# Attention in two rounded halves: value products on split probabilities, and transposed probabilities evacuated piece by piece

## The reference, cut to what matters

```
logits = einsum(q, k_selected) / 8 + bias        # float32
p      = softmax(logits)                         # over the kept keys
out    = einsum(p, v_selected)                   # 64 values per head
```

## Time and profile before

| | us |
|---|---|
| runs (three) | 911.77, 914.68, 911.13; median 911.77 |
| profiled execution | 911.06 |
| its span | 909.2 |
| TensorE busy | 876.1 (96%) |
| VectorE busy | 562.5 (62%) |
| ScalarE busy | 412.4 (45%) |
| GpSimd busy | 362.5 (40%) |

### The profile page before, as it was taken

The page is one execution under the profiler, slowest core; times in us unless marked ns, Lnnn a source line. Parts: engine busy times, 40 slices in busy tenths (PEclk is TensorE's granted clock), DMA queues, the critical chain, the costliest instruction groups (busy, mean ns, idle before and its releaser), DMA issues.

```text
span 909.2 us, 18143 instructions
## 1 busy us (share of the span) xinstructions
PE 876.1 (96%) x6495; PEld 786.8 (87%) x6495; DVE 562.5 (62%) x1119; ACT 412.4 (45%) x1204; POOL 362.5 (40%) x537
## 2 busy tenths in 40 slices
PE   4999999999999999999998999999999999998998
PEld 4989887899999899999997997676797668998998
DVE  4537777899989988899740377756553137534111
ACT  6546671335556765675445455433342225421200
POOL 1544534249542954594669241630010105401310
PEclk9999999999999999999999999999999999999999
DMA  8220212100103020312050446653135434241422
GB/s 262 68 71 20 62 36 90 47 25 24 48 24 122 31 82 25 122 42 71 24 163 13 141 123 191 155 132 105 36 93 163 122 124 152 94 126 59 134 82 71
DMA packets 79422, 81.33 MB, mean 89 GB/s; under 512 B 20234, under 2 KB 68026, under 8 KB 79082
## 3 DMA queue, kind: packets, MB, share of 16 engines
q1 hardware_dynamic: 77722, 74.97, 27.3%
q0 software_dynamic: 1616, 5.25, 2.3%
HBM read 62.85 MB, written 17.34 MB: 88 GB/s over the span
## 4 chain that ended last, share of the span: by engine, by line
PE 62%; issue 13%; DVE 8%; DMA 7%; POOL 7%; ACT 2%; SPq 1%; DVEq 0%; POOLq 0%; ACTq 0%
PE psum L1999 12%; PE psum L1132 11%; PE psum L1996 7%; PE psum L1102 7%; DMA index_keys_T<-in_cache_ikt,index_page_rows 6%; PE psum L1088 4%; PE psum L1156 3%; PE psum L1198 3%; DVE flag L1788 3%; POOL w_low L461 3%; PE psum L1895 3%; PE psum L1067 2%; PE psum L1073 2%; PE psum L1071 2%; PE psum L1879 1%
## 5 line engine op out<-in xcount | busy, mean ns | idle before, releaser
L1999 PE MATMUL psum<-w_high,xT_high 128*128 128x256 f32 x720 | 205.1, 285 | 5.4 <-ACT stage L1582 2.3
L1999 PE MATMUL psum<-w_low,xT_high 128*128 128x256 f32 x720 | 202.6, 281 | 0.0
L1999 PE MATMUL psum<-w_high,xT_low 128*128 128x256 f32 x720 | 202.3, 281 | 0.0
L1788 DVE TENSOR_SCALAR_CACHE_REDUCE flag<-scores,candidate 128x384 f16<-128x384 f32 (+2 forms) x192 | 181.7, 946 | 6.9
L461 POOL TENSOR_TENSOR w_low<-w_raw,w_high 128x256 fp32r<-128x256 f32 (+1 forms) x168 | 122.7, 766 | 72.3 <-ACT w_high L1475 63.1
L1999 PEld LDWEIGHTS psum<-w_high,xT_high 128*128 128x128 f32 x720 | 128.2, 178 | 8.3 <-ACT stage L1582 2.5
L1999 PEld LDWEIGHTS psum<-w_low,xT_high 128*128 128x128 f32 x720 | 128.4, 178 | 2.3
L1999 PEld LDWEIGHTS psum<-w_high,xT_low 128*128 128x128 f32 x720 | 128.1, 178 | 2.4
L785 ACT ACTIVATE prob<-psum,neg_max 128x1024 f32<-128x1024 f32 (+7 forms) x64 | 47.5, 742 | 131.8 <-DVE neg_max L1005 131.8
L1996 PE MATMUL psum<-xT_high,w_high 128*128 128x384 f32 (+3 forms) x312 | 102.1, 327 | 1.6 <-DVE xT_low L1715 1.2
L1996 PE MATMUL psum<-xT_high,w_low 128*128 128x384 f32 (+3 forms) x312 | 99.7, 320 | 0.0
(11 more groups left out here) (299 smaller groups left out, 1847.1 us busy)
## 6 DMA issues: line engine op xcount, KB each, us to landing
w_raw<-in_w_main SPq DMA_DIRECT2D x40, 512.0 KB, 3.8
page_keys<-in_cache_kt SPq DMA_DIRECT2D x64, 128.0 KB, 2.6
page_values<-in_cache_v SPq DMA_DIRECT2D x64, 128.0 KB, 2.2
x_rows<-in_x_prompt SPq DMA_DIRECT2D x8, 512.0 KB, 5.8
x_res<-in_x_prompt SPq DMA_DIRECT2D x32, 128.0 KB
out<-y_rows SPq DMA_DIRECT2D x32, 128.0 KB
hgate_spill<-stage SPq DMA_DIRECT2D x16, 128.0 KB
ho_spill<-ho_rows SPq DMA_DIRECT2D x4, 512.0 KB, 3.9
```

The costliest lines, as they stand in the source:

```text
L1788: dve.tensor_scalar(JK[:, 0:w], sc, threshold(k), None, op, ALU.add, accum_out=CNT[:, k:k + 1]).then_inc(s["dve_chain"], 1)
L1999: last = pe.matmul(ps(BANK[n], w, rows(i)), x[:, k, row0(i):row0(i) + rows(i)], ww[:, sl, k, 0:w], start=first, stop=final)
```

## The change

The values are loaded per 128 rows in two halves of four blocks and split into a high part (rounded to fp32r by ScalarE) and a low part (the rest, by VectorE), which lie side by side, low then high, 128 columns for a key head. The transposed probabilities are evacuated in pieces, one for each PSUM bank: for tiles 7 to 4 blocks 0 to 3 from bank 4 and the others from bank 5; for the tiles below one piece, from bank 4 or 3 by turns. For each piece ScalarE writes the high part and VectorE the low part, PSUM minus the high part. No head is shared out by parity any more. For each block TensorE multiplies the high probabilities with low and high values (128 columns) and the low probabilities with the high values (64 columns), in fp32r. Bank 7 now holds four heads, so half a tile is put out at a time: VectorE adds the two parts (a reduction) and multiplies by the inverse row sums.

For room: two probability buffers in place of three, outputs in the loop in bank 1 alone in place of 1 and 3, other addresses, the mix blocks 0 to 4 one to three heads later, and the first two mix loads wait for the value products of the upper four tiles, because the second half of the values lies where they go.

The diff, cut to its core:

```diff
@@ -70,11 +70,17 @@
 SOFT_AT = MASK_AT[-1]
 VALUES_AT = [SOFT_AT + x for x in (6, 7, 8, 9, 11, 12, 14, 15)]
 
-SHARED_FROM = SOFT_AT
+PIECES = []
+for _m in range(NT * AH):
+    _t = NT - 1 - _m // AH
+    PIECES += [(_m, 4, 0, 4), (_m, 5, 4, _t + 1)] if _t >= 4 else [(_m, (4, 3)[_m % 2], 0, _t + 1)]
...
 
 ORDER = [7, 6, 5, 4, 3, NT, 2, 1, 0]
-MIX_AT = [34, 36, 39, 42, 45, 48, 53, 60]
+MIX_AT = [37, 39, 41, 43, 46, 48, 53, 60]
 OUT_AT = [41, 43, 45, 47, 49, 51, 52, 54, 55, 58, 63]
 HIGH_AT = {35: 0, 45: 1}
 
@@ -139,7 +145,7 @@
 OUTS += [(1, 3), (1, 4), (1, 5), (0, 8), (1, 6), (1, 7), (1, 8)]
 OUTS += [(v, x) for v in (2, 3) for x in range(NT + 1)]
 IN_LOOP = len(OUT_AT)
-OBANK = [(1, 3)[y % 2] if y < IN_LOOP else (0, 2, 1, 3)[(y - IN_LOOP) % 4] for y in range(len(OUTS))]
+OBANK = [1 if y < IN_LOOP else (0, 2, 1, 3)[(y - IN_LOOP) % 4] for y in range(len(OUTS))]
 OPREV = [max([m for m in range(y) if OBANK[m] == OBANK[y]], default=-1) for y in range(len(OUTS))]
 OEND = [max(y for y, o in enumerate(OUTS) if o[0] == v) + 1 for v in range(NUO)]
...
@@ -308,7 +314,8 @@
                                ("intra", [2, 2, P], F32), ("ho_rows", [NT, P], F32))
         QD, _ = over(_e - NT * P * 4, ("q_decayed_ref", [T], F32))
         assert _e <= cur[0], (_e, cur[0])
-        AO, PB, _e = over(I0, ("attn_out", [NT + 1, 512], F32), ("prob", [3, T], F32))
+        AO, PB, PTL, _e = over(I0, ("attn_out", [NT, 512], F32), ("prob", [2, T], F32), ("pT_low", [2, NT, P], F32R))
+        assert _e <= cur[0]
...
+
+
+        VA, BH, PTH, _e = over(H0, ("values_low_high", [4, KVH, 2, HD], F32R), ("bias_high", [AH, NEAR], F32R),
+                               ("pT_high", [2, NT, P], F32R))
         assert _e <= cur[0], (_e, cur[0])
+        VB, _ = over(S0 + SCW * 2, ("values_low_high_2", [4, KVH, 2, HD], F32R))
+        VHL = (VA, VB)
+        RA, _ = over(H0, ("values_raw", [4, KVH, 2, HD], F32))
+        RB2, _ = over(S0 + SCW * 2, ("values_raw_2", [4, KVH, 2, HD], F32))
+        VRAW = (RA, RB2)
 
         PSA = ctx.enter_context(nc.psum_tensor("psum", [P, 8 * 512], F32))
...
@@ -508,6 +521,12 @@
             for g, page in enumerate(pages_):
                 sp.dma_start(KP[x][:, :, g * P:(g + 1) * P], cache_kt[bass.ds(page, 1)].rearrange("a d j k -> (a d) j k"))\
                     .then_inc(s[f"key_pages_in{x}"], 16)
+
+        def load_values(sp, half):
+
+            for b in range(4):
+                t = 4 * half + b
+                sp.dma_start(VRAW[half][:, b, :, 0, :], v_prompt[0, 0, t * P:(t + 1) * P]).then_inc(s["values_in"], 16)
 
         def sp_last_unit(sp, q):
...
@@ -559,6 +578,8 @@
 
             def load_mix(x):
                 i = ORDER[x]
+                if x == 0:
+                    sp.wait_ge(s["attn_values_done"], NA // 2)
                 ge(sp, s["mix_transposed"], 2 * (x - 1))
                 ge(sp, s["mix_attn_ready"], x - 1)
                 for dst, src in ((HOR, d_ho), (HGR, d_gh), (AGR, d_ga)):
...
@@ -584,13 +605,16 @@
                     load_res(y + 2)
 
             store_keys(sp, NT - 1)
+            sp.wait_ge(s["q_rows_transposed"], NT)
+            sp.wait_ge(s["k_rows_transposed"], NT)
+            sp.wait_ge(s["k_out0"], 16 * 4)
+            sp.wait_ge(s["k_out1"], 16 * 4)
+            load_values(sp, 1)
             for n in range(2, 2 * SB):
                 load_key_pages(sp, n)
             for x in range(4):
                 sp.wait_ge(s[f"rows_out{x}"], ALLS[x])
             sp.wait_ge(s["ho_out"], 16 * NG)
-            sp.wait_ge(s["k_out0"], 16 * 4)
-            sp.wait_ge(s["k_out1"], 16 * 4)
             for b in range(4):
                 load_value_pages(b)
             sp.wait_ge(s["sample_hgrn_normed"], 1)
...
             sp.wait_ge(s["early_outputs_stored"], 48)
+            for b in range(4, SB):
+                load_value_pages(b)
             load_mix(0)
             load_mix(1)
-            for b in range(4, SB):
-                load_value_pages(b)
             sp.wait_ge(s["sample_values_done"], SB - 1)
             load_weights(sp, NU)
...
@@ -773,26 +798,33 @@
                 elif kind == "mix":
                     mix_high(act, b)
 
+            def values_high(half):
+                act.wait_ge(s["values_in"], 64 * (half + 1))
+                act.activation(VHL[half][:, :, :, 1, :], VRAW[half][:, :, :, 0, :], ACT.Copy).then_inc(s["values_high_ready"], 1)
+
             for side in SIDE[-1]:
                 sample(*side)
+            values_high(0)
             act.wait_ge(s["ho_out"], 16 * NG)
             for m in range(NA + 1):
                 if m < NA:
                     t, h = tile(m), m % AH
                     w = P * (t + 1)
                     act.wait_ge(s["max_ready"], m + 1)
-                    ge(act, s["probs_transposed"], m - 2)
-                    act.activation(PB[:, m % 3, 0:w], ps(2 * (m % 2), w), ACT.Exp, scale=-1.0, bias=NB[:, h:h + 1],
+                    ge(act, s["probs_transposed"], sum(len(PIECES_OF[x]) for x in range(m - 1)))
+                    act.activation(PB[:, m % 2, 0:w], ps(2 * (m % 2), w), ACT.Exp, scale=-1.0, bias=NB[:, h:h + 1],
                                    accum_out=RS[:, t % 2, h:h + 1]).then_inc(s["probs_ready"], 1)
                 m1 = m - 1
-                if m1 >= 0 and not by_dve(m1):
-                    w = P * (tile(m1) + 1)
-                    act.wait_ge(s["probs_transposed"], m1 + 1)
+                for x in PIECES_OF[m1] if m1 >= 0 else ():
+                    _, bank, b0, b1 = PIECES[x]
+                    act.wait_ge(s["probs_transposed"], x + 1)
                     ge(act, s["attn_values_done"], m1 - 1)
-                    if m1 == 0:
+                    if x == 0:
                         act.wait_ge(s["final_state_out"], 32)
-                    act.activation(PTS[:, m1 % 2, :, :].rearrange("p b t -> p (b t)")[:, 0:w], ps(4, w), ACT.Copy)\
-                        .then_inc(s["probs_T_act_ready"], 1)
+                    act.activation(PTH[:, m1 % 2, b0:b1, :].rearrange("p b t -> p (b t)"), ps(bank, (b1 - b0) * P), ACT.Copy)\
+                        .then_inc(s["probs_T_high_ready"], 1)
+                if m1 == 0:
+                    values_high(1)
                 for side in SIDE.get(m1, ()) if m1 >= 0 else ():
                     sample(*side)
...
@@ -988,8 +1020,14 @@
                 elif kind == "residual":
                     add_residual(b)
 
+            def values_low(half):
+                dve.wait_ge(s["values_high_ready"], half + 1)
+                dve.tensor_tensor(VHL[half][:, :, :, 0, :], VRAW[half][:, :, :, 0, :], f(VHL[half][:, :, :, 1, :]), ALU.subtract)\
+                    .then_inc(s["values_split"], 1)
+
             for side in SIDE[-1]:
                 sample(*side)
+            values_low(0)
             for m in range(NA + 3):
                 if m - 3 == SOFT_AT:
 
...
@@ -1005,21 +1043,23 @@
                     dve.tensor_tensor_reduce(lg, lg, mask, -HD ** -0.5, 3e38, ALU.add, ALU.min, accum_out=NB[:, h:h + 1])\
                         .then_inc(s["max_ready"], 1)
                 m2 = m - 3
-                if m2 >= 0 and m2 % AH == AH - 1:
-                    t = tile(m2)
+                if m2 >= 0 and m2 % 4 == 3:
+                    t, h0 = tile(m2), m2 % AH - 3
+                    dve.wait_ge(s["probs_ready"], m2 + 1)
+                    dve.reciprocal(RI[:, h0:h0 + 4], RS[:, t % 2, h0:h0 + 4])
                     dve.wait_ge(s["attn_values_done"], m2 + 1)
-                    dve.wait_ge(s["probs_ready"], m2 + 1)
-                    link(dve.reciprocal(RI[:, :], RS[:, t % 2, :]))
-                    dve.tensor_tensor(AO[:, t, :].rearrange("p (h d) -> p h d", d=HD),
-                                      ps(7).rearrange("p (h d) -> p h d", d=HD), bc(RI[:, :], HD), ALU.mult)\
-                        .then_inc(s["attn_out_ready"], 1)
+                    ao = AO[:, t, h0 * HD:(h0 + 4) * HD].rearrange("p (h d) -> p h d", d=HD)
+                    link(dve.reduce_sum(ao, ps(7).rearrange("p (h a d) -> p h d a", a=2, d=HD), axis=AX.X))
+                    dve.tensor_tensor(ao, ao, bc(RI[:, h0:h0 + 4], HD), ALU.mult).then_inc(s["attn_out_ready"], 1)
                 m1 = m - 1
-                if 0 <= m1 < NA and by_dve(m1):
-                    w = P * (tile(m1) + 1)
-                    dve.wait_ge(s["probs_transposed"], m1 + 1)
-                    ge(dve, s["attn_values_done"], m1 - 1)
-                    dve.tensor_copy(PTS[:, m1 % 2, :, :].rearrange("p b t -> p (b t)")[:, 0:w], ps(4, w))\
-                        .then_inc(s["probs_T_dve_ready"], 1)
+                for x in PIECES_OF[m1] if 0 <= m1 < NA else ():
+                    _, bank, b0, b1 = PIECES[x]
+                    dve.wait_ge(s["probs_T_high_ready"], x + 1)
+                    high = PTH[:, m1 % 2, b0:b1, :].rearrange("p b t -> p (b t)")
```

(35 more changed lines are left out.)

23 lines of the change are left out of this document (12 added, 11 removed).

## The result

The kernel after took 965.04 us (median of 4 runs, 961.01 to 969.6) against 913.22 (4 runs, 911.13 to 915.28) for the one before, side by side: ratio 1.057, interval 1.053 to 1.062, so slower. The forecast was 957, in a range of 934 to 974. The profiled execution took 961.0 us; its span is 959.3 us, 50.1 more than before, and the prediction's sum had 45.

A forecast was written before the change was run, and what follows sets the result against it. TensorE, 96% busy, was taken to bound the kernel, with its own cost unchanged. Terms of 13+10+4+7+6+5 = 45 us on the profiled 911.1, with 0.7 to the median, gave about 957, range 934 to 974.

The forecast's parts named there:

- unevenness: Whole tail: long TensorE heads and long ring turns fall on different heads; between 0 and 12 us, taken as 5.
- the rival that ended faster: Value products: a pair of fp32r passes costs 0.17 us a block, 17 us less, about 894; chance 0.05.
- The ring: Each head's closed turn: maximum, exponential, high, low, side work; 6.85 us in rounds, 3.85 in tile 5; terms +13, +10.
- The signs given beforehand: Profile after: tile 7 heads 6.8 us apart, TensorE idle about 0.9 a head in rounds, over 1 in tile 5.
- Head 1: Before head 1, VectorE's second value split and head 0's low parts delay round 0: 1.4 to 4.6 us, taken as 3.
- the sentence that costs SyncE's queue at nothing: SP's queue: four value loads stand before key pages from number 2 on, some 2 us of issue, costed at 0.
- Rest of tile 3, and tile 2: Ring turns plus gated rows, mix low parts and residuals exceed TensorE's time: +4 and +7 us.
- late weights: First two mix loads wait for value products and stand before the output's weights: 0, up to 3 us if late.
- TensorE at 1.2 GHz: Rival, chance 0.07: TensorE at 1.2 GHz in part of the tail, or hand-overs of 0.15 us; about 980.
- Tiles 1 and 0: Outputs in bank 1 wait for residuals at heads 51/52 and 54/55, 2.9 and 1.5 us; with unevenness +6.
- No change: Rival: passes cost the same and the ring's turns stay hidden under TensorE; 911 us, chance 0.04.
- Ring half absorbed: Rival: side work sits in the gap while ScalarE works, a third to a half of 45 us; about 930, chance 0.10.

The follow-up runs named there:

- high_first: Changed kernel with ScalarE's high parts of the previous head put before the exponential of the current head; 948.43 us, ratio 1.040.
- split_later: Changed kernel with the second half of the values split one head later on both engines; 961.33 us, ratio 1.054.
- state_late: high_first with GpSimd's 2 MB of state loads waiting until the values are in; 945.54 us, ratio 1.036.
- pages_first: high_first with the second value split one head later, GpSimd's 2 MB late, key pages 2 and 3 issued before SyncE's waits; 945.85 us (937.51 to 950.09).
- best_of_change: pages_first with no two loop outputs in neighbouring heads; 934.35 us, ratio 1.022.
- before_lists_alone: Kernel before the change with only its two lists: mix blocks later, all loop outputs in bank 1; 919.98 us against 915.21, ratio 1.0055.
- before_wait_alone: Kernel before the change, ScalarE copying every head's transposed probabilities and VectorE waiting each head for the previous head's copy; 922.67 us against 912.42, ratio 1.013.
- Filler: high_first plus 5, 12 and 7 unused 512-column products on TensorE before its waits for mix blocks 0, 1 and 2; 944.23 us, ratio 1.030.
- mix_spread: high_first with mix blocks 1 to 5 one head later each; 945.63 us, ratio 1.038.
- outs_apart: high_first with loop outputs never in neighbouring heads (53, 55, 57, 59 for 52, 54, 55, 58); 942.64 us, ratio 1.032.

## Why the forecast was right, and where its terms were not

The sum was 45 us and the span grew by 50.1. The range was wider than its terms: the items named below and above the sum add up to some 12 us each (5 + 1.6 + 5.5, and 7 + 1.6 + 3, with the waits of head 1 at 4.6), not to 15 and 16, and the measured time lies inside either. A slip of no weight: it is the fourth window of the earlier trace rows, not the third, that starts inside tile 3. The terms beside what the table shows for after:

```
step                             forecast   measured
heads 0 to 11 (rounds, head 1)      13        15.4   (head 1 alone 10.4)
heads 12 to 23 (tile 5)             10         6.4
tile 4, heads 32 and 33              0         0.2
rest of tile 3                       4         6.9
tile 2                               7        12.7
tiles 1 and 0                        6         8.9
unevenness                           5         in the above
```

**TensorE's part.** Right: 0.22 us a block, inside the 0.22 to 0.24 that the 128-column row gave. The lower bound of 0.17 a block, on which the rival that ended faster stood, did not come; nor, for fp32r, did the estimate of 0.16 a block that was worked out from the Trainium skill (TensorE: Matmul & The Clock Gate, Back-to-back issue gap).

**The ring.** Shown by the timeline, and by high_first, where cutting it open gave the rounds and tile 5 back to TensorE's pace. Its length was nearly right where it can be read: 6.57 us against 6.85 in tile 7 with a round, and in tile 5, in a turn without side work (timeline of after, VectorE), 3.6 us from the maximum's start to the low parts' end, against the 3.85 forecast:

```profile
696.83 0.95 DVE L1043 CUSTOM_DVE_ANT_0 psum<-psum,mask 128x768 f32<-128x768 f32 x1
...
699.38 1.02 DVE L1059 TENSOR_TENSOR pT_low<-psum,pT_high 128x512 fp32r<-128x512 f32 x2 [1.54 <-ACT pT_high L824]
```

Its price up to head 34 was 9.8 us, not 20, and this is the term most over-sized. In the rounds a turn is 0.6 us longer than TensorE's head, not 0.9, and the loss starts late: heads 2 to 4 stay 5.97 us apart and the ring only shows from head 5 on, where the forecast had it from head 1. That VectorE and ScalarE get ahead while TensorE is held in head 1 would explain it, and is argued, not shown. The signs given beforehand came out in part: the heads of tile 7 behind the stall are 5.97 to 7.17 us apart in place of 6.8, and those of tile 6 with a round take 0.5 to 0.7 more than before.

**Head 1.** Against the +3 of the prediction this was a different thing and more than three times the size. The step of the prediction that failed is the sentence that costs SyncE's queue at nothing: it looked at the four value loads (2 us of issue) and not at the wait for the key rows' stores that the diff moves ahead of them. Three kernels show it: with the split alone moved, TensorE waits as long, for the key pages behind the same wait (split_later); with the 2 MB moved, the stores are quick and the pages slow (state_late); with pages ahead of the wait, the 2 MB behind the values and the split later, most of the stall ends in the executions that were profiled (pages_first, best_of_change). The ring's two terms were 10 us too large, head 1 was 7 too small, and tiles 3 to 0 were 11.5 too small with 5 for unevenness against it. That these errors nearly cancel is luck.

**Rest of tile 3, and tile 2.** Forecast 11, measured 19.6 us. Four things are in it. The lists alone cost 6.0 between heads 34 and 44 in the profiled execution of a kernel without any ring (before_lists_alone); this was the "late weights" of the prediction, costed at 0, up to 3. The wait for ScalarE alone costs 5.7 between the same heads, without the lists and without low parts (before_wait_alone).

The third is TensorE at 1.2 GHz, which the prediction named as a rival with 0.07, and which did come. One output of 24 products that runs at that level throughout lasts 5.1 us (24 times 0.21, in before_lists_alone) in place of 2.9 (24 times 0.12); in after the output of head 41 took 4.1, with 14 loads 0.21 apart. Filler puts the price at about 5.5 us in high_first. It came in tile 5 too, as the rival had it: behind an idle gap of 2.2 us in head 19 the loads of head 20 are 0.21 apart up to 699.4, and the granted clock is 0.83 in the mean of 690 to 700 us, where high_first has 1.00. That is 1.7 us of tile 5 (an estimate: 10 us with 0.34 of them at half speed), so the rival was right in kind and small there, and larger in the mix blocks.

The fourth are the waits in front of the mix blocks' transposes. They end with the gated rows on VectorE. In all four blocks from head 37 to head 43 TensorE's first transpose starts 0.07 or 0.08 us behind the end of L931 (780.52 behind 780.45, 790.36 behind 790.28, 800.84 behind 800.76, 812.32 behind 812.24), in high_first too, while GpSimd's gates for the same block were done some 7 us before or more. Here is the block of head 39 in after, VectorE's timeline and then the weight loads:

```profile
786.16 0.69 DVE L1059 TENSOR_TENSOR pT_low<-psum,pT_high 128x512 fp32r<-128x512 f32 x1 [2.34 <-ACT pT_high L824]
786.77 1.28 DVE L940 TENSOR_TENSOR xT_low<-psum,xT_high 128x512 fp32r<-128x512 f32 x2
787.96 1.19 DVE L930 TENSOR_TENSOR ho_in<-ho_in,ho_square_sums 128x512 f32<-128x512 f32 x1
789.19 1.09 DVE L931 TENSOR_TENSOR ho_in<-ho_in,hgate_in 128x512 f32<-128x512 f32 x1
```

```profile
790.36 0.72 PEld L1158 LDWEIGHTS psum<-ident,attn_out 128*128 128x128 f32 x4 [1.73 <-issue]
```

This is a second closed turn, through TensorE: transposes of head 38, high part, low part, low parts of the last block, gated rows, and then TensorE's own transposes of the block. The prediction had each of these in VectorE's sum for tiles 3 and 2, but in the first ring, which high_first cuts without ending these waits. It also took 1.4 us for a block's gated rows. They take 2.3 and 2.9 in heads 39 and 41, and 1.4 in heads 37 and 43: the long ones have GpSimd at work beside them, here:

```profile
786.10 1.28 POOL L706 TENSOR_TENSOR hgate_in<-hgate_in,hgrn_gain 128x512 f32<-128x512 f32 x1 [10.53 <-DMA agate_in<-agate_spill]
787.33 1.28 POOL L716 TENSOR_TENSOR attn_out<-attn_out,agate_in 128x512 f32<-128x512 f32 x1
788.56 6.44 POOL L474 TENSOR_TENSOR w_low<-w_raw,w_high 128x256 fp32r<-128x256 f32 x8
```

mix_spread moved these waits to later heads and won nothing. How the 19.6 us divide between the four stays open, as they overlap; no kernel here gave GpSimd or VectorE's side work another order, or took the mix loads' new wait away.

**Tiles 1 and 0.** Forecast +6, with bank 1 making 2.9 and 1.5 at the neighbours; heads 52 and 55 took 4.75 and 1.6 more than before, and outs_apart removed them. Right in place and kind. In before_lists_alone the same two heads cost 1.8 and 1.1, together less than half. It has no low parts ahead of the residual in VectorE's queue, and its granted clock is 1.00 in head 52 where after has 0.81; the two were not separated.

**The rivals.** "No change" and "faster" are out by the interval. "Ring half absorbed" was right on the ring's price and wrong on the time, as head 1 and the mix took its place. What is left unexplained in best_of_change, 2.2% over before, lies mostly in heads 34 to 44 (14.4 of its 25.4 us lag), where the lists, the clock and the mix meet, and in heads 0 to 4 (5.3).

## What to carry to other kernels

When a copy that one engine did becomes two halves on two engines, write down both queues and look for a closed turn; here it is cut open by swapping two instructions in one queue, worth 9.8 us up to head 34 in the profiled executions and 16.6 in the medians of the whole. Then look for the next turn, through the side work. Follow each wait that a diff moves on a DMA queue to everything that is issued behind it, and not only the transfers that it was written for; and before a large load is moved, see what it will then run beside. A stall costs twice when the engine behind it comes back at a lower clock, and moving a deadline in a packed list of work mostly moves the wait.

## What the runs showed of the hardware

- An fp32r product of 64 columns goes no faster than one of 128: both 0.11 us from load to load, so taking half the columns of the low product saved nothing.
- The granted clock of TensorE fell to 0.53 in the mean of 780 to 804 us after, its 1.2 GHz level for nearly all of that time, behind idle gaps of 0.7 and 2.1 us in head 37 and with TensorE busy 20.2 of those 24 us. Before, the clock was 1.00 in all of the tail. With the waits filled by products it stayed at 1.00 from head 34 to head 44.
- With 2 MB of loads on another queue beside them the last store of key rows (128 KB) landed 10.7 us behind its issue and kept SyncE waiting 10.0 us in after, 10.4 and 9.7 in high_first; without them 2.4 and 1.6 (state_late). The key pages (128 KB a load) took up to 11.1 us with the same 2 MB beside them and 2.4 or 2.5 without.
- VectorE's product of two SBUF tiles, 128x512, took 0.68 or 0.69 us where GpSimd was idle, and 1.09 to 1.63 in the two blocks of after where a GpSimd operation ran beside it; the low parts of the block, 128x512 from PSUM, kept their pace beside it (two in 1.28 us). Not each is slowed: in high_first one took 0.68 us (at 776.33) beside a GpSimd operation that took 1.75 in place of 1.28.
